# Two-layer hybrid decoder: one dense step of the sparse-attention layer is split over two turns

## The chip, the cores and the metric

The kernel runs on one core of a Trainium2 chip. The metric is the device time of one execution in microseconds (us); lower is better.

## The reference

The input x is 512 tokens by 1024 features in float32, with two layers. Each layer is x = x + norm(mixer(norm(x))), then x = x + norm(mlp(norm(x))), with RMS norms and a squared-ReLU MLP of width 4096. The mixer of layer 0 is sliding-window attention with sinks. The mixer of layer 1, where the change lies, is attention over selected keys:

```python
proj = h @ w_in
q, k, v, qi, ki, wi = jnp.split(proj, B_SPLITS, axis=-1)     # 16 query heads, 4 key heads of 64
...
score = jnp.einsum('bths,bth->bts', jax.nn.relu(logits), wi_blk.astype(jnp.float32))
score = jnp.where(key_pos[None, None, :] <= t[None, :, None], score, -jnp.inf)
_, idx = lax.top_k(score, n_sel)                             # 128 keys for each query
...
pr = jax.nn.softmax(s, axis=-1)
return jnp.einsum('bhgtk,btkhd->bthgd', pr.astype(v_sel.dtype), v_sel)
...
return out @ w_out
```

## The kernel before, in words

Every engine (PE, ACT, DVE, POOL, SP) has a program written out by hand, and semaphores alone tie them together. Precision is kept by splitting each operand of a dense product into a high and a low part (`hi`, `lo`); one product is then three matmuls (`hi*hi`, `hi*lo`, `lo*hi`).

**Weights.** A weight unit is 512 rows by 512 columns. SP loads it into `w_raw`, ACT writes its high part (`split`, or `split_half` at L915 in two halves), and DVE or POOL (`split_low`, L804) writes the low part. A unit's place is free for a later unit when its last reader on PE has signalled. For units with an even number within their stage that signal is the semaphore `first_half_done`, sent by the last matmul of the dense step of token block j = 3. Units 58 and 59 are the two halves (rows 0 to 511 and 512 to 1023) of the last query columns of layer 1; units 60 to 63 are its output projection. ACT's high part of unit 60 goes where that of unit 58 lies, so `split_half(60, 0)` waits for `first_half_done` from the last dense step that reads unit 58. SP loads unit 62 when POOL has finished the low part of unit 60.

**Dense steps.** A dense step is one token block of 128 by one weight unit: `dense` issues 12 matmuls of 128x512 (L1998, L1999, L2000), three for each of four values of k. It can be cut: `fill(s, ks)` does only the values of k in ks, and the step's signal is sent only with k = 3.

**Turns.** Attention runs in 16 turns of four heads each, numbered 0 to 15 (two more close the pipeline). In PE's turn n stand, in this order: the transposes of the probabilities of turn n-1 (L2192), the scores of turn n+1 (`by_rows`, L2137), the weighted sums of turn n-2 (L2206), the turning of later queries if any (L2117), and the dense steps that the table `FILL` names for the turn. The other engines keep step: DVE masks the scores (`masked`, L1440) and finds the row maximum, ACT takes exponents (`expo`, L1032), DVE takes reciprocals of the row sums (`inverse`, L1447), POOL multiplies (`normed`, L783), PE transposes, ACT copies to SBUF (`pt_copy`, L1039), PE sums. In layer 1 DVE also runs the rounds of the key selection between these (MAX8 at L1523 and MATCH_REPLACE8 at L1528).

In layer 1 the first turns have one key block (128 keys) each: turns 0 to 3. Turns 4 to 7 have 256 keys. `FILL[1]` gives turns 0, 1 and 3, 4 of layer 1 the dense steps 0, 1, 2, 3, and turn 2 none. Steps 0 and 1 multiply token blocks 2 and 3 by unit 58, and steps 2 and 3 the same blocks by unit 59.

**ACT in its turn n** does, in order: the copies of turn n-1; the second half of a split begun in turn n-1 (`split_half(u, 1)`); the high parts of turned queries (L1014); the exponents of turn n+1; `o_high` (L1044) in odd turns from 3; the scaling of a finished dense result (`q_scaled`, L1004); and the first half of a split that the table `SPLITS` names. For layer 1, `SPLITS` is:

```python
{1: (60,), 4: (61,), 5: (62,), 6: (63,)}
```

So `split_half(60, 0)` is the last thing in ACT's turn 1, and behind it, in turn 2, stand `pt_copy` of turn 1, `split_half(60, 1)`, and `expo` of turn 3.

**DVE in its turn n** does: `masked` for turn n+1, the low parts of turned queries (L1387), a selection round over 512 keys, `inverse` of turn n+1, in odd turns from 3 `o_low` (L1453), and a selection round over 384 keys.

**POOL in its turn n** does `normed` of turn n, then half of the low part of a POOL unit: for unit 60, k = 0 and 1 in turn 2 and k = 2 and 3 in turn 3.

Of the kernel before, what the change touches and what calls it, by code (L numbers as in the profile page):

```python
# [127 lines left out]
def turn(layer, n):  # L128
    p, i = PAIRS[layer][n // 2]
    return p, i, n % 2  # L130
# [12 lines left out]
def pt_of(layer, n):  # L143
    return range(PT_AT[16 * layer + n], PT_AT[16 * layer + n + 1])
# [4 lines left out]
FILL_IN = (12, 20)  # L149
FILL = ({-1: (0, 1), 0: (2, 3), 1: (4,), 2: (5,), 3: (6,), 4: (7,), 5: (8,), 6: (9,), 7: (10,), 8: (11,),  # L150
         10: (12, 13), 11: (14, 15), 12: (16, 17), 13: (18, 19), 14: (20,), 15: (21,)},
        {0: (0,), 1: (1,), 3: (2,), 4: (3,), 6: (4,), 7: (5,), 8: (6,), 9: (7,), 10: (8,), 11: (9,), 12: (10,), 13: (11,),
         14: (12,), 15: (13,)})

Q_TURN = ({-1: ((1, 0), (1, 1)), 1: ((1, 2),), 2: ((1, 3),), 4: ((2, 0),), 6: ((2, 1),), 8: ((2, 2),), 10: ((2, 3),)},
# [13 lines left out]
HALVED = (8, 9, 60, 61, 62, 63)  # L169

FILL_OUT = (12, 4)


def in_step(layer, s):

    return s // 8, (s % 4) // 2, 2 * ((s % 8) // 4) + s % 2


def q_no(layer, c, j):


    return 4 * (c - 1) + j if not layer else 7 + 4 * c + j
# [73 lines left out]
def hybrid_trunk(nc, x, x_turned, positions, gains, gains_turned, w_up, w_down, a_in, a_out, sinks, b_in, b_out, consts, out):  # L256
# [4 lines left out]
    with ctx:  # L261
# [305 lines left out]
        def width(layer, i):  # L567
            return len(key_blocks(layer, i)) * P
# [155 lines left out]
        def _(pool):  # L724
# [107 lines left out]
            for layer in range(DEPTH):  # L832
# [26 lines left out]
                for n in range(-1, 17):  # L859
# [17 lines left out]
                    for s in FILL[layer].get(n, ()):  # L877
                        if s < FILL_OUT[layer]:
                            c, h, j = in_step(layer, FILL_IN[layer] + s)
                            if h and n not in ROPED_LATER[layer]:  # L880
                                rope_q(q_no(layer, c, j))
                        else:
                            j, c, h = (s - FILL_OUT[layer]) // 4, (s - FILL_OUT[layer]) % 4 // 2, s % 2
                            if h and c:
# [11 lines left out]
        def _(act):  # L896
# [150 lines left out]
            def attention(layer):  # L1047
                norm = 2 * layer + 1
                for n in range(-1, 17):
# [29 lines left out]
                    for s in FILL[layer].get(n, ()):  # L1079
                        if s < FILL_OUT[layer]:  # L1080
                            c, h, j = in_step(layer, FILL_IN[layer] + s)
                            if h and (layer, n, j) != (0, 0, 2):
                                q_scaled(layer, c, j)
                        else:
                            j, c, h = (s - FILL_OUT[layer]) // 4, (s - FILL_OUT[layer]) % 4 // 2, s % 2
                            if h:
# [245 lines left out]
        def _(dve):  # L1332
# [123 lines left out]
            def attention(layer, others):  # L1456
                norm = 2 * layer + 1
                pending = []
                for n in range(-1, 17):
# [6 lines left out]
                    for s in FILL[layer].get(n - 1, ()):  # L1466
                        if s >= FILL_OUT[layer]:
                            j, c, h = (s - FILL_OUT[layer]) // 4, (s - FILL_OUT[layer]) % 4 // 2, s % 2
                            if h:
# [467 lines left out]
        def _(pe):  # L1937
# [103 lines left out]
            def in_work(layer, s, ks=(0, 1, 2, 3)):  # L2041
                c, h, j = in_step(layer, s)
                u = U[f"in{layer}"] + 2 * c + h
                if j == 0 and ks[0] == 0:
                    pe.wait_ge(*low_of(u))
                if c == 0:
                    pe.wait_ge(h_lo, h_no(2 * layer, j, h) + 1)
                ins = dense(u, h, layer, d_no(layer, "in", c, j), in_reg(layer), j, ks)
                if ks[-1] < 3:
                    return  # L2050
                if h:
                    ins.then_inc(d_done, 1)
                elif j == 3:
                    ins.then_inc(first_half_done, 1)
# [24 lines left out]
            def out_work(layer, j, c, h, ks=(0, 1, 2, 3)):  # L2079
                u = U[f"out{layer}"] + 2 * c + h  # L2080
                if ks[0] == 0:
                    if j == 0:
                        pe.wait_ge(*low_of(u))
                    if h == 0 and c == 0:
                        pe.wait_ge(o_lo_done, 8 * layer + max(pair_of(layer, p, j) for p in range(2)) + 1)
                ins = dense(u, h, layer, d_no(layer, "out", c, j), q_reg(layer), j, ks)
                if ks[-1] < 3:
                    return
                if h:
                    ins.then_inc(d_done, 1)  # L2090
                elif j == 3:
                    ins.then_inc(first_half_done, 1)

            def new_x(norm, j):

                layer = norm // 2
                pe.wait_ge(x_new, 8 * (norm - 1) + 2 * j + 2)
                for h in range(2):
                    bank = t_free(layer, ("h", norm, j, h))
                    if norm == 2 and j == 0:  # L2100
                        pe.wait_ge(tile_out, LAYER_TILES - 4)
                    for k in range(4):
                        ins = nc.tensor.transpose(bank[:, blk(k)], X[:, j, blk(4 * h + k)], ident[:, 0:P])
                    ins.then_inc(h_t, 1)
# [8 lines left out]
            def queries_turned(layer, qn):  # L2113
                bank = t_free(layer, ("q", qn))
                pe.wait_ge(q_roped, qn + 1)
                for r in range(4):
                    ins = nc.tensor.transpose(bank[:, blk(r)], qs[:, qn % 2, blk(r)], ident[:, 0:P])  # L2117
                ins.then_inc(q_t, 1)
# [66 lines left out]
            def transposes(layer, n, c):  # L2185
                N = 16 * layer + n
                K = PT_AT[N] + c
                bank = t_free(layer, ("pt", K))
                if c == 0:
                    pe.wait_ge(p_done, 4 * N + 4)  # L2190
                for e in range(4):
                    ins = nc.tensor.transpose(bank[:, blk(e)], probs[:, N % 3, e, blk(c)], ident[:, 0:P])  # L2192
                ins.then_inc(pt_ready, 1)
# [17 lines left out]
            def attention(layer):  # L2211
                norm = 2 * layer + 1

                def fill(s, ks=(0, 1, 2, 3)):
                    if s < FILL_OUT[layer]:
                        in_work(layer, FILL_IN[layer] + s, ks)
                    else:
                        m = s - FILL_OUT[layer]
                        out_work(layer, m // 4, m % 4 // 2, m % 2, ks)

                def turned(n):
                    for c, j in Q_TURN[layer].get(n, ()):
                        queries_turned(layer, q_no(layer, c, j))
                    for j in H_TURN[layer].get(n, ()):
                        new_x(norm, j)

                def scores_of(n):
                    scores(layer, n, 0)
                    if width(layer, turn(layer, n)[1]) <= 256:
                        scores(layer, n, 1)  # L2230

                for n in (-1, 0):
                    steps = FILL[layer].get(n, ())
                    for s in steps[:1]:
                        fill(s)
                    if n == -1:
                        turned(n)
                        for s in steps[1:]:
                            fill(s)
                    scores_of(n + 1)  # L2240
                    if n == 0:
                        turned(n)
                        for s in steps[1:]:
                            fill(s)
                for n in range(1, TURNS + 2):
                    turning = len(pt_of(layer, n - 1)) if n - 1 < TURNS else 0
                    summing = len(pt_of(layer, n - 2)) if n >= 2 else 0
                    wide = n + 1 < TURNS and width(layer, turn(layer, n + 1)[1]) > 256
                    second = wide or turning > 2 or summing > 2
                    for c in range(min(turning, 2)):  # L2250
                        transposes(layer, n - 1, c)
                    if n + 1 < TURNS:
                        scores_of(n + 1)
                    for c in range(min(summing, 2)):
                        weighted(layer, n - 2, c)
                    turned(n)
                    steps = FILL[layer].get(n, ())
                    for s in steps[:-1]:
                        fill(s)
                    if steps:  # L2260
                        fill(steps[-1], (0, 1) if second else (0, 1, 2, 3))
                    if second:
                        for c in range(2, turning):
                            transposes(layer, n - 1, c)
                        if wide:
                            scores(layer, n + 1, 1)
                        for c in range(2, summing):
                            weighted(layer, n - 2, c)
                        if steps:
                            fill(steps[-1], (2, 3))  # L2270
# [143 lines left out]
            for s in range(8, 12):  # L2414
                in_work(0, s)
                keys_turned(0, s - 8)
            attention(0)
            out_tail(0)
            mlp(0)
# [85 lines left out]
```

## Time and profile before

| what | value |
|---|---|
| median of 3 runs | 1081.02 us (1080.26 to 1081.09) |
| profiled execution, its own time | 1083.11 us |
| span of the profiled execution | 1081.3 us |
| PE busy | 1059.2 us (98%) |
| DVE / ACT / POOL busy | 747.6 / 539.6 / 189.5 us |
| mean granted TensorE clock | 0.996 |

The span runs from the first to the last instruction of the trace. Timeline rows give the start of a group of instructions, its length, and in brackets how long the engine stood idle before it and what released it.

### The profile page before, as it was taken

What the parts mean: (1) busy time and instruction counts of PE and PEld (TensorE: products, weight loads), DVE (VectorE), ACT (ScalarE), POOL (GpSimd) and SP (SyncE); (2) the same over time, 40 slices, a digit from 0 to 9 for tenths busy, and PEclk for the clock granted to TensorE, in tenths of its full rate; (3) what the DMA queues carried; (4) which work ended last, traced back from release to release, by engine and by line L of the source; (5) the groups of instructions that cost most, each with busy time, mean ns of one, the idle gap of its engine ahead of it and who ended that gap; (6) DMA issues with size and microseconds to landing.
All of it is one profiled execution on the core that took longest, in us unless ns stands there. A gap on an engine that the chain in (4) does not pass through costs nothing.

```text
span 1081.3 us, 14860 instructions
## 1 busy us (share of the span) xinstructions
PE 1059.2 (98%) x5408; PEld 860.9 (80%) x5408; DVE 747.6 (69%) x1284; ACT 539.6 (50%) x1017; POOL 189.5 (18%) x331
## 2 busy tenths in 40 slices
PE   9999999999999999999999989999999999999997
PEld 8777779888888888888777766679888888888885
DVE  5455545586697697687578889536596697696684
ACT  6577545354444454425553567645354453453422
POOL 0365420000000000005403367520000000000005
PEclk9999999999999999999999989999999999999999
DMA  9531505635445455332623333005544535535502
GB/s 293 120 78 40 118 1 118 136 79 117 93 103 118 86 109 117 81 75 50 135 42 78 78 78 80 1 1 131 124 100 95 116 80 117 113 83 117 110 8 78
DMA packets 52009, 99.94 MB, mean 92 GB/s; under 512 B 4704, under 2 KB 4832, under 8 KB 51936
## 3 DMA queue, kind: packets, MB, share of 16 engines
q1 hardware_dynamic: 51216, 98.61, 40.4%
q8 instruction: 43, 0.70, 0.3%
q10 hardware_dynamic: 720, 0.38, 0.1%
q14 instruction: 30, 0.25, 0.1%
HBM read 96.88 MB, written 2.10 MB: 92 GB/s over the span
## 4 chain that ended last, share of the span: by engine, by line
PE 89%; DVE 5%; DMA 2%; ACT 2%; issue 1%; SPq 1%; POOL 0%; POOLq 0%; DVEq 0%; ACTq 0%
PE bank L1988 11%; PE bank L1990 11%; PE bank L1989 11%; PE bank L2347 7%; PE bank L2348 7%; PE bank L2349 7%; PE bank L1998 6%; PE bank L2000 6%; PE bank L1999 6%; PE bank L2137 3%; PE bank L2373 3%; PE bank L2372 3%; PE bank L2371 3%; PE bank L2206 2%; PE bank L2192 2%; DMA w_raw<-in_a_w_in 2%
## 5 line engine op out<-in xcount | busy, mean ns | idle before, releaser
L1988 PE MATMUL bank<-r_hi,w_hi 128*128 128x512 f32 (+1 forms) x456 | 177.5, 389 | 0.0
L1989 PE MATMUL bank<-r_hi,w_lo 128*128 128x512 f32 (+1 forms) x456 | 177.4, 389 | 0.0
L1990 PE MATMUL bank<-r_lo,w_hi 128*128 128x512 f32 (+1 forms) x456 | 177.4, 389 | 0.0
L1587 DVE TENSOR_TENSOR w_lo<-w_raw,w_hi 128x1024 fp32r<-128x1024 f32 x84 | 102.0, 1222 | 71.2 <-ACT w_hi L1124 71.2
L1124 ACT ACTIVATE w_hi<-w_raw 128x1024 fp32r<-128x1024 f32 x84 | 87.9, 1056 | 120.5 <-PE bank L1990 82.9
L2347 PE MATMUL bank<-w_hi,hid_hi 128*128 128x512 f32 x336 | 130.7, 389 | 0.0
L2348 PE MATMUL bank<-w_lo,hid_hi 128*128 128x512 f32 x336 | 130.7, 389 | 0.0
L2349 PE MATMUL bank<-w_hi,hid_lo 128*128 128x512 f32 x336 | 130.7, 389 | 0.0
L1133 ACT ACTIVATE w_hi<-w_raw,gT 128x512 fp32r<-128x512 f32 x96 | 64.6, 716 | 105.8 <-DMA w_raw<-in_w_mlp_up 74.3
L791 POOL TENSOR_TENSOR acc<-acc,G 128x512 f32<-128x512 f32 x8 | 13.0, 1651 | 594.3 <-ACT waste L984 594.3
L1990 PEld LDWEIGHTS bank<-r_lo,w_hi 128*128 128x128 f32 (+1 forms) x456 | 85.2, 187 | 18.2
L1989 PEld LDWEIGHTS bank<-r_hi,w_lo 128*128 128x128 f32 (+1 forms) x456 | 85.2, 187 | 18.0
L1988 PEld LDWEIGHTS bank<-r_hi,w_hi 128*128 128x128 f32 (+1 forms) x456 | 85.2, 187 | 18.0
L783 POOL TENSOR_TENSOR probs<-probs,small 128x256 f32<-128x256 f32 (+3 forms) x128 | 82.0, 673 | 75.3 <-DVE small L1447 75.0
L1998 PE MATMUL bank<-w_hi,r_hi 128*128 128x512 f32 x208 | 86.7, 417 | 2.7 <-DVE w_lo L1365 2.1
L1668 DVE SCALAR_TENSOR_TENSOR w_lo<-w_raw,gT,w_hi 128x512 fp32r<-128x512 f32 x96 | 68.2, 746 | 27.5 <-ACT w_hi L1133 27.5
L2000 PE MATMUL bank<-w_hi,r_lo 128*128 128x512 f32 x208 | 82.1, 395 | 0.0
L1999 PE MATMUL bank<-w_lo,r_hi 128*128 128x512 f32 x208 | 82.0, 394 | 0.0
L1032 ACT ACTIVATE probs<-probs,small 128x257 f32<-128x257 f32 (+5 forms) x128 | 65.4, 517 | 22.8 <-DVE small L1440 22.7
L2349 PEld LDWEIGHTS bank<-w_hi,hid_lo 128*128 128x128 f32 x336 | 63.1, 188 | 13.1
L2347 PEld LDWEIGHTS bank<-w_hi,hid_hi 128*128 128x128 f32 x336 | 63.1, 188 | 13.1
L2348 PEld LDWEIGHTS bank<-w_lo,hid_hi 128*128 128x128 f32 x336 | 63.1, 188 | 13.1
(209 smaller groups left out, 2152.6 us busy)
## 6 DMA issues: line engine op xcount, KB each, us to landing
w_raw<-in_w_mlp_up SPq DMA_DIRECT2D x64, 512.0 KB, 6.4
w_raw<-in_w_mlp_down SPq DMA_DIRECT2D x64, 512.0 KB, 6.9
w_raw<-in_b_w_in SPq DMA_DIRECT2D x16, 512.0 KB, 6.7
w_raw<-in_a_w_in SPq DMA_DIRECT2D x8, 512.0 KB, 8.4
w_raw<-in_a_w_out SPq DMA_DIRECT2D x8, 512.0 KB, 5.8
w_raw<-in_b_w_out SPq DMA_DIRECT2D x8, 512.0 KB, 6.1
xt<-in_x_turned SPq DMA_DIRECT2D x8, 256.0 KB, 5.7
X<-in_x SPq DMA_DIRECT2D x4, 512.0 KB, 11.3
```

The source lines that it names most:

```text
L783: nc.gpsimd.tensor_tensor(v, v, inv_sum[:, N % 3, c:c + 1].to_broadcast([P, W]), ALU.mult).then_inc(p_done, 1)
L1124: nc.scalar.activation(half_of(w_hi[:, u % 2, :], a), b_of(name, a), ACT.Copy).then_inc(b_hi_done, 1)
L1587: nc.vector.tensor_tensor(half_of(w_lo[:, u % 2, :], a), b_of(PRODUCTS[i][1], a), half_of(w_hi[:, u % 2, :], a).bitcast(f32), ALU.subtract ...
L1988: nc.tensor.matmul(bank, whi, xhi, start=start, stop=False)
L1989: nc.tensor.matmul(bank, wlo, xhi, start=False, stop=False)
L1990: return nc.tensor.matmul(bank, whi, xlo, start=False, stop=stop)
L1998: nc.tensor.matmul(bank[:], xh, hi[:, k, :], start=h == 0 and k == 0, stop=False)
L1999: nc.tensor.matmul(bank[:], xh, lo[:, k, :], start=False, stop=False)
L2000: ins = nc.tensor.matmul(bank[:], xl, hi[:, k, :], start=False, stop=h == 1 and k == 3)
L2347: nc.tensor.matmul(bank[:], xh[:, k, blk(j)], hi[:, k, :], start=k == 0, stop=False)
L2348: nc.tensor.matmul(bank[:], xh[:, k, blk(j)], lo[:, k, :], start=False, stop=False)
L2349: ins = nc.tensor.matmul(bank[:], xl[:, k, blk(j)], hi[:, k, :], start=False, stop=k == 3)
```

## The change

Dense step 1 of layer 1 leaves the table `FILL` and is done in two pieces instead: k = 0 and 1 at its old place in turn 1, k = 2 and 3 at the end of turn 2. Layer 0 gets an empty table. The other engines' programs stay as they were, since step 1 has no scaling and no rotation behind it.

```diff
@@ -149,7 +149,7 @@
-        {0: (0,), 1: (1,), 3: (2,), 4: (3,), 6: (4,), ...
+        {0: (0,), 3: (2,), 4: (3,), 6: (4,), ...
@@ -169,6 +169,8 @@
 FILL_OUT = (12, 4)
+
+FILL_PARTS = ({}, {1: (1, (0, 1)), 2: (1, (2, 3))})
@@ -2254,6 +2256,8 @@
                         weighted(layer, n - 2, c)
                     turned(n)
+                    if n in FILL_PARTS[layer]:
+                        fill(*FILL_PARTS[layer][n])
                     steps = FILL[layer].get(n, ())
                     for s in steps[:-1]:
                         fill(s)
```

## Rows read from the trace of the kernel before

**Rows 1.** The page, part 1: busy time of each engine.

```profile
PE 1059.2 (98%) x5408; PEld 860.9 (80%) x5408; DVE 747.6 (69%) x1284; ACT 539.6 (50%) x1017; POOL 189.5 (18%) x331
```

**Rows 2.** Timeline of PE, layer 1, turns 1 and 2.

```profile
614.04 0.50 PE L1998 MATMUL bank<-w_hi,r_hi 128*128 128x512 f32 x1
...
616.99 0.63 PE L2192 MATMUL bank<-ident,probs 128*128 128x128 f32 x4
...
620.91 0.63 PE L2192 MATMUL bank<-ident,probs 128*128 128x128 f32 x4 [1.70 <-POOL probs L783]
```

**Rows 3.** Windows; after the engines' busy times: PE clock, DMA, GB/s.

```profile
620.00:622.00 2.00, 0.96 (x6) 0.79 (x8) 1.96 (x10) 2.00 (x8) 1.84 (x4) 0.86 0.00 0
622.00:624.00 2.00, 2.00 (x16) 1.31 (x14) 1.90 (x7) 0.87 (x4) 2.00 (x4) 0.50 0.03 8
...
628.00:630.00 2.00, 2.00 (x17) 1.56 (x17) 1.24 (x4) 0.81 (x2) 2.00 (x5) 0.93 0.58 130
```

**Rows 4.** Timeline of PE, layer 1, turns 3 to 5.

```profile
621.66 0.58 PE L2137 MATMUL bank<-k_hi,r_hi 64*128 64x256 f32 x2
...
624.29 0.80 PE L1998 MATMUL bank<-w_hi,r_hi 128*128 128x512 f32 x1
...
628.99 0.60 PE L2192 MATMUL bank<-ident,probs 128*128 128x128 f32 x4
629.52 0.39 PE L2137 MATMUL bank<-k_hi,r_hi 64*128 64x256 f32 x2
...
631.01 0.50 PE L1998 MATMUL bank<-w_hi,r_hi 128*128 128x512 f32 x1
...
633.89 1.03 PE L2192 MATMUL bank<-ident,probs 128*128 128x128 f32 x8
```

**Rows 5.** Timeline of DVE, layer 1, turns 2 to 5.

```profile
622.95 0.18 DVE L1447 RECIPROCAL small<-small 128x4 f32<-128x4 f32 x1
...
624.26 0.48 DVE L1440 CUSTOM_DVE_ANT_0 probs<-bank,score,small 128x256 f32<-128x256 f32 x1
...
630.70 0.48 DVE L1440 CUSTOM_DVE_ANT_0 probs<-bank,score,small 128x256 f32<-128x256 f32 x1 [1.43 <-PE bank L2137]
...
636.03 0.49 DVE L1440 CUSTOM_DVE_ANT_0 probs<-bank,score,small 128x256 f32<-128x256 f32 x1 [0.91 <-PE bank L2137]
...
638.16 0.69 DVE L1387 TENSOR_TENSOR r_lo<-bank,r_hi 128x512 fp32r<-128x512 f32 x1 [0.43 <-ACT r_hi L1014]
```

**Rows 6.** Timeline of POOL, layer 1, turns 1 to 4.

```profile
615.37 1.48 POOL L783 TENSOR_TENSOR probs<-probs,small 128x128 f32<-128x128 f32 x4 [3.03 <-DVE small L1447]
...
620.92 2.51 POOL L804 TENSOR_TENSOR w_lo<-w_raw,w_hi 128x512 fp32r<-128x512 f32 x2 [0.16 <-ACT w_hi L915]
...
627.65 2.33 POOL L783 TENSOR_TENSOR probs<-probs,small 128x256 f32<-128x256 f32 x4 [0.29 <-DVE small L1447]
```

**Rows 7.** Timeline of ACT, layer 1, turns 1 to 7.

```profile
618.38 1.04 ACT L915 ACTIVATE w_hi<-w_raw 128x1024 fp32r<-128x1024 f32 x1
619.32 0.57 ACT L1039 ACTIVATE pt<-bank 128x512 f32<-128x512 f32 x1
...
620.75 0.39 ACT L1032 ACTIVATE probs<-probs,small 128x128 f32<-128x128 f32 x1
...
622.20 0.19 ACT L1032 ACTIVATION_READ_ACCUMULATOR probs<-probs,small 128x1 f32 x1
...
634.09 0.69 ACT L1004 ACTIVATE qs<-bank,small 128x512 f32<-128x512 f32 x1 [0.78 <-PE bank L2000]
...
640.45 1.06 ACT L915 ACTIVATE r_hi<-w_raw 128x1024 fp32r<-128x1024 f32 x1
...
650.05 1.06 ACT L915 ACTIVATE r_hi<-w_raw 128x1024 fp32r<-128x1024 f32 x1 [2.65 <-DMA w_raw<-in_b_w_out]
651.01 1.07 ACT L1039 ACTIVATE pt<-bank 128x512 f32<-128x512 f32 x2
```

**Rows 8.** The page, part 6: loads of the output projection's units.

```profile
w_raw<-in_b_w_out SPq DMA_DIRECT2D x8, 512.0 KB, 6.1
```

More of the change, by code:

```diff
@@ L151 @@
          10: (12, 13), 11: (14, 15), 12: (16, 17), 13: (18, 19), 14: (20,), 15: (21,)},
-        {0: (0,), 1: (1,), 3: (2,), 4: (3,), 6: (4,), 7: (5,), 8: (6,), 9: (7,), 10: (8,), 11: (9,), 12: (10,), 13: (11,),
+        {0: (0,), 3: (2,), 4: (3,), 6: (4,), 7: (5,), 8: (6,), 9: (7,), 10: (8,), 11: (9,), 12: (10,), 13: (11,),
          14: (12,), 15: (13,)})
```

## Prediction

> **What bounds the kernel now.** I read the page first. PE is busy 98% of the span [rows 1], so a change to the order of PE's own work can win only idle time of PE or time at a lower clock. The timeline of PE then shows both around the place of the change. After the weighted sums of turn 2 PE stands idle for 1.70 us, from 619.21 to 620.91, until POOL has the probabilities of turn 2 [rows 2]. Right behind that hole the granted clock is 0.86 in one stretch and 0.50 in the next, which is the lower of its two levels, 1.2 GHz, and by 628 to 630 it is back at 0.93 [rows 3]. Before it fell, the engine had done only transposes, scores and sums of the narrow turns and had then been idle; before it rose it had run the dense step of turn 3. The dip costs PE this: scores and sums of turn 3 take 624.29 - 621.66 = 2.63 us, and the same work in turn 4 at full clock 631.01 - 629.52 = 1.49; the dense step takes 628.99 - 624.29 = 4.70 us against 633.89 - 631.01 = 2.88 [rows 4]. Together 2.96 us.
>
> Then the timelines of the engines that feed PE. POOL starts turn 1's multiplication at 615.37, released by DVE [rows 6], and DVE works without a gap from there to 629.27, where it first waits for PE: 1.43 us before 630.70, then 0.91 us before 636.03, then 0.43 us for ACT before 638.16 [rows 5]. So in turns 1 to 3 DVE sets the pace, and from turn 4 PE, late by its slow clock, holds DVE. Those three waits, 2.77 us, are all that DVE could give back before 638.16.
>
> **What moves.** Six of the step's twelve matmuls. At full clock half a step is 2.88 / 2 = 1.44 us [rows 4]. The instructions are the same in number, no DMA is issued, and nothing moves past SP's or POOL's queue. What moves with the second half is its signal `first_half_done`.
>
> *PE, turn 1.* The first half runs from 614.04 to about 615.5 [rows 2]. The transposes need POOL, whose multiplication ends at 615.37 + 1.48 = 616.85 [rows 6]; they start at 616.99 in either order [rows 2]. So a new hole of about 1.5 us opens in turn 1, and nothing is won there: the matmuls that left were hiding POOL.
>
> *PE, turn 2.* The second half starts at 619.15 to 619.2 and PE is free again at about 620.64; the transposes stay at 620.91, since POOL's multiplication of turn 2 hangs on DVE. The hole shrinks from 1.70 to about 0.3 us and again no time is won directly. What could be won is the dip behind it. I take it that the dip goes, since six dense matmuls now stand right ahead of the place where the clock fell.
>
> *ACT.* This is the cost. `split_half(60, 0)` starts at 618.38 now, without waiting [rows 7]. It will wait for the last moved matmul: that starts at 619.15 + 5 x 0.24 (12 matmuls in 2.88) = 620.4 and lasts 0.4, so ACT starts it at about 620.84, 2.46 us late. Behind it in the queue stand the copy of turn 1 (619.32 becomes 621.78), the second half of the split, and the exponents of turn 3 (620.75 becomes 623.21) [rows 7]. The exponents' last reading ends at 622.39 now and at 624.85 then. The copy ends at 622.35; its reader, the sums in turn 3, comes after scores that start at 621.66 and take about 0.9 at full clock, so PE does not wait for it.
>
> *DVE.* `inverse` of turn 3, now at 622.95 [rows 5], has a slack of 0.56 and so comes at about 624.88, 1.93 us late. DVE is the pace-maker here, so all behind it moves: the mask of turn 4 from 624.26 to 626.19.
>
> *POOL.* The low part of unit 60 waits for the split, so it goes from 620.92 to 623.38 and ends at about 625.86; the multiplication of turn 3, 1.48 us, stands behind it and ends at 627.3; the other half of the low part, 2.5 us, ends at 629.83; then turn 4's multiplication of 2.33 us ends at 632.16 [rows 6].
>
> *SP.* The load of unit 62 follows POOL's low part: issued at 629.8 instead of 627.4, landed 6.1 us later [rows 8] at about 636, and its reader is at 640.45 [rows 7]. Some 4 us of cover: it costs nothing, and would cost one for one beyond that.
>
> *Downstream.* At full clock PE is through turn 3 at 621.66 + 1.49 + 2.88 = 626.03 instead of 628.99, but waits for POOL until 627.44: a third hole, 1.4 us. The scores of turn 5 are done about 629, and turn 4's dense step runs from 629.46 to 632.5 instead of to 634.05. DVE is ready for the mask of turn 5 at 629.27 + 1.93 = 631.20 instead of 630.70, so of its 1.43 us wait nothing is left and 0.50 is lost. The mask of turn 6, before which it had waited 0.91, comes at 635.62 instead of 636.03. ACT's scaling, 634.09 and released by PE [rows 7], now follows the exponents of turn 5, which end 0.50 later than now; that puts it at 633.71, 0.38 early, and what hangs on it (L1387 on DVE at 638.16) is 0.38 early too. From there DVE, the output steps and PE's full turns follow in a fixed chain. The sum: -2.77 (waits of DVE) +1.93 (ACT's hold) +0.46 (what ACT's order keeps) = -0.38 us.
>
> The profiled execution took 1083.11 us (1081.3 of span, 1.8 around it), so it would take 1082.7. The median of the runs shown is 2.09 below it; I carry the difference over: 1081.02 - 0.38 = **1080.6 us**.
>
> **Bounds of what no row shows.** Whether the clock stays up cannot be read from this trace. With no dip after the change, the term is as above. If it falls after the new hole in turn 1, see rival 2. Whether the timed runs have the dip at all is open too: without it L1387 would follow ACT's scaling, which would follow the exponents of turn 5; masks at 629.3 and those exponents' end near 631.9 put L1387 at about 636.0, so the dip is worth 638.16 - 636.0 = 2.17 us. See rival 3.
>
> **A rule against the change.** At 650.05 ACT waits 2.65 us for a transfer, and the copies behind it start only at 651.01 [rows 7], although PE's transposes of that turn lay well before. So I charge everything behind the held split. The Trainium skill, TensorE: Matmul & The Clock Gate, section "Architectural detail: the array is 16x 32x32, not 1x 128x128", says that the queues of ScalarE and VectorE are strictly first in, first out and that only TensorE pulls anything ahead. By that rule the hold passes on whole, as in the sum; if ready work could go past the split, the sum would be that of rival 1. The rows agree with it.
>
> **Rivals.**
>
> 1. *The hold costs nothing.* The dip goes and ACT's work behind the split is still in time: all 2.17 us are won, 1078.85 us. It decides if the exponents of turn 3 come less than 0.56 us late. Against it: the 2.46 us above. Chance 0.06, the only case near "faster".
>
> 2. *The dip moves.* The clock falls after the new hole of 1.5 us in turn 1. For it: that hole is nearly as long as the old one, and again narrow transposes and scores follow. Against it: dense matmuls stand close on both sides. Price: scores, sums and half a step of turn 2 stretch by the ratios in [rows 4], some 0.6 + 0.5 + 1.15 = 2.2 us, so the signal and ACT are 4.7 us late, `inverse` of turn 3 4.1 us. Less 1.43, the mask of turn 5 is 2.7 late, and ACT's scaling about 2.3 late: 1083.3 us. This one ends slower; from the point where a fall of the clock delays the signal at all, it decides. Chance 0.20.
>
> 3. *The timed runs have no dip.* Then before is already 2.17 us better than its profile, and the change brings only the hold: 2.17 - 0.38 = 1.8 us slower, 1082.8 us. For it: the profiled execution is 2.09 us above the median, near the price of the dip. Against: recording may itself take that. Chance 0.27; with rival 2 on top, some 4.5 us slower, 1085.5, another 0.04.
>
> 4. *The change does nothing*: signal and holes as before. Excluded by the signal's place in `in_work`.
>
> **How the numbers follow.** The forecast has 0.43. 0.2% is 2.2 us, about what a measurement of this kernel can tell from no change. Faster: rival 1 and little else, 0.05. Slower: rivals 2 and 3 with 2 on top, and part of rival 3, whose 1.8 us lies near the bound: 0.29. Same: 0.66. The range leaves out rival 1 and the double case: 1079.6 to 1083.8.
>
> **What would show it.** In the profile after: a PE hole of 1.5 us before the transposes at 616.99 and one of 0.3 at 620.91; `w_hi` L915 idle about 2.4 us before 620.84 and released by PE; RECIPROCAL of turn 3 near 624.9, released by ACT; no stretch at clock 0.50; PE waiting 1.4 us for POOL near 627.4; L1387 near 637.8. The prediction is wrong if the clock still falls, or if the timed runs of before never had the dip.

## The result: 0.19% slower, where 0.04% faster was forecast as the likeliest

| | before | after |
|---|---|---|
| median | 1080.87 us (17 runs, 1080.26 to 1083.14) | 1083.29 us (17 runs, 1081.82 to 1084.81) |
| profiled execution | 1083.11 us, span 1081.3 | 1083.06 us, span 1081.3 |

The ratio after to before is 1.0019, with a 95% interval of 1.0013 to 1.0026, which is 1.4 to 2.8 us. (This ratio and those below are taken from all executions of the two kernels, not from their medians; the quotient of the two medians is slightly different, 1.0022.) The forecast was 1080.6 us with a range of 1079.6 to 1083.8: the time lies in the range, but the change made the kernel slower, and 0.38 us faster was named as likeliest. The two profiled executions are of equal length, so a comparison of these two alone shows no loss at all. That is the trap of this case.

The page after, part 1, and windows of the clock (PE, PEld, DVE, ACT, POOL busy, then clock, DMA, GB/s), answers to [rows 1, 3]:

```profile
PE 1058.4 (98%) x5408; PEld 859.8 (80%) x5408; DVE 747.9 (69%) x1284; ACT 539.1 (50%) x1017; POOL 190.0 (18%) x331
```

```profile
620.00:622.00 2.00, 1.76 (x15) 1.15 (x15) 1.93 (x11) 1.27 (x2) 0.59 (x2) 1.00 0.00 0
622.00:624.00 2.00, 2.00 (x16) 1.32 (x14) 0.74 (x2) 2.00 (x7) 0.71 (x1) 1.00 0.02 4
...
638.00:640.00 2.00, 1.48 (x8) 1.16 (x10) 1.93 (x5) 2.00 (x9) 0.45 (x1) 0.59 0.03 8
640.00:642.00 2.00, 2.00 (x18) 1.51 (x18) 2.00 (x1) 2.00 (x5) 0.00 (x0) 0.56 0.00 0
```

The dip behind turn 2 is gone, and PE's busy time is 0.8 us less; a shorter dip, 3.4 us long, stands at 638.4 to 641.8.

Timeline of PE after the change, turns 1 to 3 and 6, the rows with a wait and the dense steps' first matmuls (answers to [rows 2, 4]):

```profile
613.87 0.50 PE L2000 MATMUL bank<-w_hi,r_hi 128*128 128x512 f32 x1
...
616.81 0.63 PE L2194 MATMUL bank<-ident,probs 128*128 128x128 f32 x4 [1.28 <-POOL probs L785]
...
618.97 0.50 PE L2000 MATMUL bank<-w_hi,r_hi 128*128 128x512 f32 x1
...
620.73 0.63 PE L2194 MATMUL bank<-ident,probs 128*128 128x128 f32 x4
...
627.42 0.63 PE L2194 MATMUL bank<-ident,probs 128*128 128x128 f32 x4 [1.42 <-POOL probs L785]
...
638.52 1.12 PE L2194 MATMUL bank<-ident,probs 128*128 128x128 f32 x4 [0.81 <-DVE r_lo L1389]
```

All starts are 0.18 us earlier than in the profile of before, since attention of layer 1 began that much earlier. Allowing for it, the transposes of turns 1 and 2 did not move: the hole was carried from turn 2 into turn 1, and a new one of 1.42 us stands before 627.42.

Timeline of ACT after, answers to [rows 7]:

```profile
620.73 1.06 ACT L917 ACTIVATE w_hi<-w_raw 128x1024 fp32r<-128x1024 f32 x1 [2.43 <-PE bank L2002]
621.69 0.58 ACT L1041 ACTIVATE pt<-bank 128x512 f32<-128x512 f32 x1
...
623.11 0.40 ACT L1034 ACTIVATE probs<-probs,small 128x128 f32<-128x128 f32 x1
...
640.07 1.06 ACT L917 ACTIVATE r_hi<-w_raw 128x1024 fp32r<-128x1024 f32 x1
```

Timeline of DVE after, answers to [rows 5]; the first and the last row are the reciprocals of turns 0 and 15:

```profile
610.42 0.18 DVE L1449 RECIPROCAL small<-small 128x4 f32<-128x4 f32 x1 [0.90 <-ACT probs L1034]
...
624.85 0.18 DVE L1449 RECIPROCAL small<-small 128x4 f32<-128x4 f32 x1 [2.11 <-ACT probs L1034]
...
626.17 0.48 DVE L1442 CUSTOM_DVE_ANT_0 probs<-bank,score,small 128x256 f32<-128x256 f32 x1
...
631.22 0.48 DVE L1442 CUSTOM_DVE_ANT_0 probs<-bank,score,small 128x256 f32<-128x256 f32 x1
...
635.67 0.48 DVE L1442 CUSTOM_DVE_ANT_0 probs<-bank,score,small 128x256 f32<-128x256 f32 x1
...
637.77 0.69 DVE L1389 TENSOR_TENSOR r_lo<-bank,r_hi 128x512 fp32r<-128x512 f32 x1 [0.40 <-ACT r_hi L1016]
...
708.41 0.18 DVE L1449 RECIPROCAL small<-small 128x4 f32<-128x4 f32 x1 [0.92 <-ACT probs L1034]
```

Timeline of POOL after, turns 2 and 3, answers to [rows 6]:

```profile
623.29 2.55 POOL L806 TENSOR_TENSOR w_lo<-w_raw,w_hi 128x512 fp32r<-128x512 f32 x2 [2.71 <-ACT w_hi L917]
625.79 1.48 POOL L785 TENSOR_TENSOR probs<-probs,small 128x128 f32<-128x128 f32 x4
```

ACT is held by PE's moved matmuls, and DVE and POOL by ACT. The waits that PE's slow clock had caused on DVE before the masks of turns 5 and 6 [rows 5] are gone; a wait of 2.11 us for ACT stands in their place.

**The stretch.** From the last reciprocal to the end of the span it is 372.8 or 372.9 us in every profile of this study. What a kernel does to the time therefore shows in the stretch from turn 0's reciprocal to turn 15's: 708.41 - 610.42 = 98.0 us after, and 97.9 in the profile of before. The experiments are read by it. What lies ahead of it varied by up to 4 us between profiles: its first row starts between 609.25 and 613.34. The three latest starts (612.35, 612.72 and 613.34) belong to the three profiles in which the clock fell for 3.4 us near the start of the program, between 31 and 42 us; in the eleven others it did not fall before the stretch, and the stretch starts between 609.25 and 610.90.

### The profile page after: what moved, and what is told of

The parts are those of the page before. It is cut to its first block, busy times and chain, and to the rows that moved or that the text cites. A ratio compares the mean times of both kernels' runs of the same rounds, so it can differ in the third digit from the quotient of the medians.

```text
span 1081.3 us, 14860 instructions
## 1 busy us (share of the span) xinstructions
PE 1058.4 (98%) x5408; PEld 859.8 (80%) x5408; DVE 747.9 (69%) x1284; ACT 539.1 (50%) x1017; POOL 190.0 (18%) x331
## 4 chain that ended last, share of the span: by engine, by line
PE 86%; DVE 5%; ACT 3%; DMA 3%; issue 1%; POOL 1%; SPq 1%; POOLq 0%; DVEq 0%; ACTq 0%
PE bank L1990 11%; PE bank L1992 11%; PE bank L1991 11%; PE bank L2351 7%; PE bank L2352 7%; PE bank L2353 7%; PE bank L2000 6%; PE bank L2002 5%; PE bank L2001 5%; PE bank L2377 3%; PE bank L2376 3%; PE bank L2375 3%; PE bank L2139 3%; PE bank L2208 2%; DMA w_raw<-in_a_w_in 2%; PE bank L2194 2%
```

## The experiments

Theory A: ACT's hold behind the signal, passed to DVE, is the loss; the profile of before had a costly clock dip that most timed executions lack. Rival C: PE's new hole in turn 1, or a dip there, is the loss. Rival B: all executions of before have the dip, and recording adds the 2.1 us.

**The kernel before, once more** (no edit).

> The kernel before, once more, for the clock of each execution. Theory A (the profiled execution of before had a dip of the clock after turn 2 that most timed executions do not have; the dip costs about 2.2 us): executions fall into a large group near 1080.8 with a mean clock close to 0.999 and a small one near 1083 with a lower clock, and a profile that falls in the large group shows no stretch at clock 0.50 near 621 us and L1387 about 2.2 us earlier than 638.16. Rival B (all executions have the dip, and recording adds 2.1 us): the profile shows the dip again and its own time is near 1083 while timed ones are 1080.9; no relation of time to clock.

Measured: ratio 0.9999 (0.9991 to 1.0008), profiled execution 1080.40 us. Its hole on PE before the transposes of turn 2, and its clock in windows (busy times of PE, PEld, DVE, ACT, POOL, then clock, DMA, GB/s):

```profile
619.82 1.08 PE L2192 MATMUL bank<-ident,probs 128*128 128x128 f32 x4 [1.70 <-POOL probs L783]
```

```profile
618.00:620.00 2.00, 0.30 (x3) 0.21 (x2) 1.93 (x9) 2.00 (x5) 1.64 (x5) 0.94 0.00 0
620.00:622.00 2.00, 2.00 (x14) 1.67 (x15) 1.93 (x9) 1.78 (x9) 2.00 (x2) 0.50 0.01 4
622.00:624.00 2.00, 2.00 (x13) 1.05 (x10) 1.93 (x9) 0.29 (x1) 2.00 (x6) 0.71 0.01 4
```

Its timeline of DVE, the ends of the stretch and the wait for PE:

```profile
609.50 0.18 DVE L1447 RECIPROCAL small<-small 128x4 f32<-128x4 f32 x1 [0.91 <-ACT probs L1032]
...
633.23 0.48 DVE L1440 CUSTOM_DVE_ANT_0 probs<-bank,score,small 128x256 f32<-128x256 f32 x1 [0.58 <-PE bank L2137]
...
705.75 0.18 DVE L1447 RECIPROCAL small<-small 128x4 f32<-128x4 f32 x1 [0.92 <-ACT probs L1032]
```

The dip is there, at the same hole, but lasts about 3.4 us (619.8 to 623.2) instead of 6.8, and costs DVE one wait of 0.58 us instead of two with 2.34. The stretch is 96.2 us. So Theory A's "no dip" missed: there is a short one. Rival B falls: a profiled execution can take 1080.40 us, so recording does not add 2 us. The two groups of executions that Theory A named, one near a mean clock of 0.999, are not there either. Longer executions do tend, weakly, to have a lower mean clock: of the 101 executions of this kernel in the experiments, the 18 at 0.994 or 0.995 took 1082.8 us on average, the 55 at 0.996 took 1081.05 and the 23 at 0.997 took 1081.5. But this number cannot tell the long dip from the short one. Both profiled executions show 0.996, since low clock at the very end of the program (from about 1079 us in the first, 1074 us in the second) enters the mean as well.

**Hold alone**, on the kernel before: matmuls at their old places, ACT made to wait, before the split of unit 60, for PE's transposes of turn 2.

```diff
+                        if u == 60:
+                            act.wait_ge(pt_ready, PT_AT[16 * layer + 2] + 1)
                         if u in HALVED:
                             split_half(u, 0)
```

> The kernel before with all matmuls at their old places, and one more wait on ACT: the first half of the split of unit 60 waits for the transposes of turn 2 on PE (in PE's turn 3, about 0.7 us after the moved matmuls of the change would have ended). No hole in turn 1, the hole of turn 2 as before. Theory A (ACT's hold is the cause, whatever PE does): ACT idles about 3.1 us before the split, DVE about 2.6 us before the reciprocal of turn 3, the stretch between the first and the last reciprocal is 98.4 us (98.2 to 98.8) and the ratio to before 1.0022 (1.0010 to 1.0032). Rival C (PE's hole in turn 1 is what costs): stretch 96 to 98 as before, ratio 1.0000.

Measured: 1.0020 (1.0011 to 1.0029), stretch 98.4 us. ACT's wait is the expected 3.1 us, and DVE's row of turn 3 stands between the two ends of the stretch:

```profile
621.88 1.06 ACT L915 ACTIVATE w_hi<-w_raw 128x1024 fp32r<-128x1024 f32 x1 [3.10 <-PE bank L2194]
```

```profile
610.90 0.18 DVE L1449 RECIPROCAL small<-small 128x4 f32<-128x4 f32 x1 [0.91 <-ACT probs L1032]
...
626.01 0.18 DVE L1449 RECIPROCAL small<-small 128x4 f32<-128x4 f32 x1 [2.78 <-ACT probs L1032]
...
709.26 0.18 DVE L1449 RECIPROCAL small<-small 128x4 f32<-128x4 f32 x1 [0.92 <-ACT probs L1032]
```

With no hole in turn 1, the loss of the change is there. The old hole of turn 2 stands too (1.69 us), with a dip of 3.4 us behind it, as in the second profile of before.

**The change without the hold**: the split behind the exponents of turn 3.

```diff
+                    if (layer, n) == (1, 2):
+                        split_half(60, 0)
+                        split_half(60, 1)
...
-                            split_low(u, (2, 3))
+                            split_low(u, (0, 1, 2, 3) if u == 60 else (2, 3))
```

(and the old places of the unit's halves on ACT and of k = 0, 1 on POOL skipped)

> The change, with ACT's two halves of the split of unit 60 put behind the exponents of turn 3 (end of ACT's turn 2), and POOL's low part of unit 60 done in one piece behind its multiplication of turn 3, so that the load of unit 62 goes out no later than with the change. Theory A (the loss is what stood behind the held split): the 2.0 us wait of DVE before the reciprocal of turn 3 is gone, the stretch between the first and the last reciprocal is 95.8 us instead of 98.0, ratio to before 1.0000 (0.9990 to 1.0010). Rival C (the loss comes from PE's new hole in turn 1): the hole is still there, ratio stays at 1.0019.

Measured: 0.9997 (0.9988 to 1.0006), stretch 95.8 us. PE still has its hole in turn 1:

```profile
619.10 0.63 PE L2199 MATMUL bank<-ident,probs 128*128 128x128 f32 x4 [1.29 <-POOL probs L785]
```

and DVE's reciprocal of turn 3 waits for nothing:

```profile
625.07 0.18 DVE L1454 RECIPROCAL small<-small 128x4 f32<-128x4 f32 x1
```

This and the run before it are the pair that settles the cause: the hold without the new hole loses, and the new hole without the hold does not. In this profile the clock did not fall behind the new hole; a profile where it did, also without a hold, comes with the later split below.

**The dose.** The whole step in turn 2, `FILL_PARTS = ({}, {2: (1, (0, 1, 2, 3))})`, and only k = 3 there, `{1: (1, (0, 1, 2)), 2: (1, (3,))}`.

> The change driven further: all of dense step 1 in turn 2. Signal first_half_done and with it the split on ACT come another 1.4 us later (six more matmuls of 0.24). Theory A (the hold is passed on one for one): 1083.3 + 1.4 = 1084.7 (1084.2 to 1085.5), DVE's wait before the reciprocal of turn 3 about 3.5 us. Rival C (the hole in turn 1 alone does it): the hole in turn 1 grows to 2.9 us and turn 2 has none; 1083.3 or, if each microsecond of the hole counted, 1084.7 too, told apart by DVE's wait.

> The change made smaller: k = 0 to 2 in turn 1 and only k = 3 in turn 2. The signal comes 0.7 us earlier than with the change, at about 620.1, but still from turn 2. Theory A: 1083.3 - 0.7 = 1082.6 (1082.0 to 1083.0), DVE's wait about 1.4 us: most of the loss comes with three matmuls. Rival C: the hole in turn 1 falls by half, so the loss falls by half: 1082.1.

| kernel | DVE's wait before the reciprocal of turn 3 | stretch | ratio (95%) |
|---|---|---|---|
| k = 3 in turn 2 | 1.44 us | 97.0 us | 1.0006 (0.9998 to 1.0015) |
| the change | 2.11 us | 98.0 us | 1.0019 (1.0013 to 1.0026) |
| all in turn 2 | 7.00 us | 102.6 us | 1.0057 (1.0045 to 1.0070) |

The stretch follows the wait: against 95.8 without hold, 1.2, 2.2 and 6.8 us for waits of 1.44, 2.11 and 7.00. The small dose fits in the profile but came out 1.1 us cheaper in the median than expected (1081.51 against 1082.6, of 11 executions). That is nearer to Rival C's 1082.1, and its interval takes in no change at all, so it is the profile that speaks for the hold here. The large dose missed by more: 1086.53 us (5 executions) against 1084.2 to 1085.5, and the wait is twice the forecast 3.5 us:

```profile
629.02 0.18 DVE L1449 RECIPROCAL small<-small 128x4 f32<-128x4 f32 x1 [7.00 <-ACT probs L1034]
```

PE had stood 2.87 us before the transposes of turn 1, and from 614.0, still within this hole, to 624.3 the clock was low:

```profile
614.00:616.00 2.00, 0.00 (x0) 0.00 (x0) 1.90 (x8) 0.08 (x1) 1.47 (x4) 0.51 0.00 0
...
620.00:622.00 2.00, 2.00 (x6) 1.52 (x6) 1.97 (x9) 0.00 (x0) 0.00 (x0) 0.50 0.00 0
```

So rival 2 of the prediction, the dip that moves to turn 1, is real at this dose: it stretches the very matmuls that ACT waits for.

**The change once more** (no edit).

> The kernel after the change once more, beside the others of this set, for a second profile and the spread of its executions. Theory A: DVE's wait of 2.0 us before the reciprocal of turn 3 is there again and the stretch from the first reciprocal of this layer to the last takes 97.8 to 98.2 us, with or without a dip of the clock; the ratio to before is 1.0019 again (1.0013 to 1.0026). Rival (the loss hangs on where a dip falls): the stretch differs by more than 0.5 us between the two profiles.

Measured: 1.0017 (1.0007 to 1.0026). The profile is not that of the first time. PE before and after the hole, and DVE's wait:

```profile
616.34 0.63 PE L2194 MATMUL bank<-ident,probs 128*128 128x128 f32 x4 [1.29 <-POOL probs L785]
...
618.84 0.80 PE L2000 MATMUL bank<-w_hi,r_hi 128*128 128x512 f32 x1
```

```profile
625.92 0.18 DVE L1449 RECIPROCAL small<-small 128x4 f32<-128x4 f32 x1 [3.66 <-ACT probs L1034]
```

```profile
618.00:620.00 2.00, 2.00 (x7) 1.08 (x8) 1.90 (x8) 0.00 (x0) 1.36 (x4) 0.52 0.00 0
620.00:622.00 2.00, 2.00 (x9) 1.43 (x7) 1.97 (x11) 0.20 (x1) 0.11 (x1) 0.62 0.00 0
```

The stretch is 99.25 us: the expectation of 97.8 to 98.2 fell. Here the clock fell for 3.4 us behind the new hole (618.1 to 621.5), the half step in turn 2 ran slowly, and ACT's hold and DVE's wait grew by 1.55 us (ACT's from 2.43 to 3.98). So what rival 2 describes also happens to the change itself, in some executions. Five profiles have half of step 1 in turn 1 and so this hole of 1.28 to 1.30 us: the clock fell behind it in two (this one, and the change with the later split) and not in three (the first of the change, the split behind the exponents, and the swap below).

**Who carries it: one swap on DVE.** The change, with the selection round of turn 2 ahead of the reciprocal.

```diff
+                    if (layer, n) == (1, 2):
+                        others(n, 2)
                     if n + 1 < TURNS:
                         inverse(layer, n + 1)
```

(and its old place in that turn skipped)

> The change as it is, with one swap on DVE in turn 2: the selection round over 384 keys (1.3 us) stands before inverse of turn 3 instead of behind it, so DVE does it while it waits for the exponents. ACT's hold, PE's order and POOL's order are those of the change. Theory A (the loss reaches the end through DVE's idle time): about 1.2 us comes back, 1082.1 (1081.7 to 1082.6). Rival E (it reaches the end through POOL, whose multiplication of turn 3 is held behind the low part of unit 60, or through PE): nothing comes back, 1083.3.

Measured: 1.0005 (0.9993 to 1.0018); the median, 1080.88 us, lies below the 1081.7 to 1082.6 expected. DVE's wait is 0.87 us, the stretch 96.6 us, 1.4 less than with the change (1.2 expected), with ACT held as long (2.44 us) and POOL's order unchanged. The path is ACT, DVE, end; rival E falls. The intervals of this run and of the change overlap, so the profile has to carry this verdict:

```profile
626.81 0.18 DVE L1449 RECIPROCAL small<-small 128x4 f32<-128x4 f32 x1 [0.87 <-ACT probs L1034]
```

**A later split, with and without the change**: `SPLITS` of layer 1 begins unit 60 in turn 2 (`{2: (60,), ...`).

> The change, with the split of unit 60 begun one turn later (ACT's turn 2), so that it no longer waits for the moved matmuls and nothing of turn 2 stands behind it. Theory A (the loss of 2.4 us is ACT's hold, carried by the exponents of turn 3 and inverse on DVE): the loss is gone, 1080.9 (1080.3 to 1081.5), DVE's wait of 2.1 us before 624.85 is gone. Rival C (the loss comes from the new hole in turn 1 or from the clock, not from ACT): stays at 1083.3.

> The kernel before with the split of unit 60 begun one turn later and nothing else: the cost of the later split alone. Theory A: 1080.9, within 0.5 us of before, since POOL, the load of unit 62 and its reader have slack. If the later split has a price of its own (ACT or POOL in turns 3 and 4), it shows here, up to 1.5 us, and the first experiment of the pair has to be read against this one.

Both lost, 1.0033 (1.0021 to 1.0046) and 1.0044 (1.0031 to 1.0057), with five executions of each, so the later split has a price of its own, larger than expected, and the forecast that the loss would be gone missed. ACT's timeline in the first of them shows it:

```profile
641.64 1.06 ACT L917 ACTIVATE r_hi<-w_raw 128x1024 fp32r<-128x1024 f32 x1 [2.89 <-DMA w_raw<-in_b_w_out]
```

POOL's second half of unit 60 stands a turn later, SP's load of unit 62 is behind it, and ACT waits for that load (3.38 us in the other kernel). Read as a pair, with stretches of 98.6 and 99.0 us, the moved matmuls cost nothing where ACT is not held by them. That holds although in the first of them the clock fell for 3.4 us behind the new hole of turn 1 (618.8 to 622.2): its reciprocal of turn 3 waits for nothing, and the 2.11 us wait of the change is gone. The stretches account for 2.4 and 2.7 us of the loss against the second profile of before, the ratios for 3.6 and 4.8; the rest is not explained.

**The hole filled from the other side**: half of dense step 2, which has no such signal, goes from turn 3 to turn 2.

```diff
+FILL_PARTS = ({}, {2: (2, (0, 1)), 3: (2, (2, 3))})
...
+                    if n in FILL_PARTS[layer]:
+                        fill(*FILL_PARTS[layer][n])
-                    steps = FILL[layer].get(n, ())
+                    steps = FILL[layer].get(n, ()) if n not in FILL_PARTS[layer] else ()
```

> The kernel before with the hole of turn 2 filled from the other side: dense step 1 stays whole in turn 1, and the first half (k = 0, 1) of dense step 2 goes from turn 3 to turn 2. The step has no signal first_half_done, so ACT is not held. Theory A: the hole of 1.7 us falls to 0.3, no time is won where there was no dip since DVE sets the pace (1080.8, 1080.2 to 1081.3), but the slower executions with the dip disappear. Rival D (PE's hole in turn 2 is itself worth time): 1079.4, 1.4 us faster.

Measured: 1.0000 (0.9989 to 1.0011), stretch 95.8 us, no clock below 0.99 anywhere in the attention of layer 1. The hole and the dip are gone, and nothing was to be had: rival D falls. That the longer times would vanish is not shown: they ran from 1079.70 to 1083.15 us.

**A version that might win**: the same, and one selection round of 1.25 us done ahead of attention (`top_rounds(2, 10)`, `ROUNDS_2` one round ahead); and that round alone on the kernel before.

> The hole of turn 2 filled from step 2 as before, and one selection round over 384 keys (1.25 us of DVE) done ahead of attention, where DVE waits 1.29 us for PE, instead of in turn 5. If DVE sets the pace of turns 1 to 6 (theory A), this takes about 1.2 us off the stretch: 94.6 us instead of 95.8, ratio 0.9989 (0.9980 to 0.9998). If PE or ACT set it, nothing changes (1.0000).

> The kernel before with the early selection round alone, dense steps as before. Theory A: up to 1.2 us faster where the clock stays up, less where the slow clock makes PE the pace-maker in turns 3 to 5: stretch 95.0 to 96.7 us, ratio 0.9992 (0.9983 to 1.0002). With the kernel of step 2 and round beside it this tells what filling the hole adds once DVE is relieved.

Measured: 0.9993 (0.9984 to 1.0002) and 1.0000 (0.9991 to 1.0008); stretches 95.8 and 96.6 us, where 94.6 was expected of the first: it missed by the whole 1.2 us. The round alone gained nothing, against 0.9992 expected, and neither kernel is told from before. With both, the reciprocal of turn 7 does come 1.2 us earlier (34.4 us into the stretch instead of 35.6 with step 2 alone), but the next waits for ACT, and ACT for the load of unit 63:

```profile
652.36 0.18 DVE L1449 RECIPROCAL small<-small 128x4 f32<-128x4 f32 x1 [1.53 <-ACT probs L1034]
```

```profile
646.89 1.06 ACT L917 ACTIVATE r_hi<-w_raw 128x1024 fp32r<-128x1024 f32 x1 [3.93 <-DMA w_raw<-in_b_w_out]
```

DVE sets the pace to turn 5 or 6, not beyond.

## Why the prediction was wrong, and where it was right

**Right, step by step, for the execution it was worked out on.** 0.18 us are added to the rows of after, since its stretch began that much earlier. The hole of turn 1 (1.5 us forecast with its queueing, 1.28 by the row), that of turn 2 (0.3 forecast, no wait worth a note), ACT's split at 620.84 (620.73 + 0.18 = 620.91), the reciprocal of turn 3 at 624.88 (624.85 + 0.18 = 625.03), the hole before the transposes of turn 3 (1.4; 1.42), the mask of turn 5 at 631.20 (631.22 + 0.18 = 631.40), L1389 at 637.8 (637.77 + 0.18 = 637.95). So of the 0.38 us to be won by then, 0.21 came. It did not last: the clock fell again in turn 6, at the reciprocal of turn 8 the change is 0.07 us late, and at the last one 0.12. Unit 62's reader did not wait for its load, as forecast; the price beyond the cover was then seen in the two kernels with the later split.

**The step that failed is the one from the profile to the timed runs**: "I carry the difference over". The sum has the term -2.77 us for DVE's waits behind the slow clock. That term belongs to an execution with a dip of 6.8 us. In the second profile of the kernel before, whose execution took exactly the median of its set (1080.40), the dip is half as long, DVE's wait for PE is 0.58 us, and the stretch is 96.2 instead of 97.9 us. The change takes away at most the 0.4 us that this leaves (96.2 against 95.8 without dip) and puts 2.2 us in its place: 97.99 - 96.25 = 1.7 us slower. This is rival 3 with its price, 1.8 us, and nearly its condition: a short dip where it said none. The price of the long dip, 2.17 us in the prediction, is 97.9 - 95.8 = 2.1 by the profiles.

That the long dip is the exception is borne out in two more ways. Five profiles have PE's order of turns 1 and 2 as before, with the hole of 1.69 or 1.70 us: the dip behind it lasted 6.8 us in one (the first of before), 3.4 us in three (the second of before, the hold alone, the early round alone), and in one (before with the later split) there was none. And the ratios of the timed runs fit a stretch of 96.2 us for before, not one of 97.9. Against 96.2 the stretches give +2.1 us for the hold alone, +6.3 for all of step 1 in turn 2, +0.8 for k = 3 there and +0.3 for the swap; the ratios give 2.2, 6.2, 0.6 and 0.5. Against 97.9 the stretches would give 0.5, 4.7, -0.8 and -1.3. Each of these stretches is from one profile.

The dip was also not all of the 2.09 us between profile and median: the first profile of before started its stretch 1.1 us later than the second, for a reason ahead of it that is not known.

**The rest.** 1.7 us lie inside the interval of the ratio, 1.4 to 2.8 us, and are seven tenths of the 2.4 between the medians. What rival 2 describes may account for more: in one of two profiles of the change the clock fell behind the new hole, and the stretch took 1.3 us longer (99.25 against 97.99). How often it does so in timed runs is not known, and that this makes up the missing 0.7 us is argued, not shown. Rival 2's own price, 1083.3 us, is the measured median almost to the digit, and that is luck: it was added to an execution of before with the long dip, and in the profile where its dip came the reciprocal of turn 3 was 3.6 us late, not 4.1, and the stretch 1.4 us longer than in the first profile of before, not 2.3. That the time lies inside the range is owed to rivals 2 and 3, for whose sake it reached to 1083.8, and not to the sum. "I take it that the dip goes" held for the place behind turn 2 in the first profile; in the same profile the clock fell for 3.4 us from 638.4 on, among the holes of turn 6.

**The rule against the change.** The Trainium skill (TensorE: Matmul & The Clock Gate, "Architectural detail: the array is 16x 32x32, not 1x 128x128") states that the queues of ScalarE and VectorE are strictly first in, first out. The traces agree: a hold of 2.43 us before the split put the exponents behind it 2.36 us later in the trace (623.11 against 620.75 [rows 7]), 2.5 with the 0.18 added. They had been ready to run: taken from behind the hold, in the kernel with the split behind the exponents, they cost nothing.

**The reasons given** were right on the cause: the hold of ACT through its queue, DVE as carrier, and the move of six matmuls as worth nothing by itself. What was weighed wrongly was the evidence on which case the timed runs are in. The profiled execution was 2.09 us above a median whose three runs lay within 0.83 us, and the forecast price of the dip was 2.17: the two numbers nearly agreed, and the case built on them got a chance of 0.27 against 0.43.

## What to carry to other kernels

A dense step that fills a hole may carry a signal: before half of it is moved, ask who waits for its last matmul and what stands behind that wait in its queue. Filling PE's idle time is worth nothing where another engine sets the pace; look for who releases the instruction after the hole. And when a profiled execution is longer than the timed median by about the price of an accident seen in it, work out the change for an execution without the accident.

## What the runs showed of the hardware

The granted TensorE clock fell to its lower level (1.2 GHz) in the attention of layer 1 behind some of PE's holes, and not behind the same hole in every execution.

| hole on PE | profiles with it | clock |
|---|---|---|
| 1.69 or 1.70 us, turn 2 | 5 | low for 6.8 us in one, 3.4 us in three, not at all in one |
| 1.28 to 1.30 us, turn 1 | 5 | low for 3.4 us in two, not at all in three |
| 2.87 us, turn 1 (all of step 1 in turn 2) | 1 | low for 10.2 us, from within the hole |
| 1.42 to 1.49 us before the transposes of turn 3 | 4 | never low |

It also fell in three profiles among the short holes of turn 6 (0.40 to 0.99 us), for 3.4 us in two (the first of the change, k = 3 in turn 2) and 6.8 us in one (all in turn 2), and in the second profile of the change, the hold alone and the swap it did not. The 1.70 us hole follows narrow sums, the 1.28 us one follows six dense matmuls, and the one of 1.42 to 1.49 us, behind which the clock never fell, follows a whole dense step of twelve; narrow transposes come after all three. What decides between a fall and none, and between 3.4 and 6.8 us, no run here shows.

Where another engine sets the pace a dip of 3.4 us cost 0.4 us and one of 6.8 us 2.1 us (stretches of 96.2 and 97.9 us against 95.8 without dip). Where the slow matmuls carried a signal that others waited for, 3.4 us of it made the wait 1.55 us longer.
